# 32-bit matmuls with few moving columns, issued as two matmuls of 64 stationary columns each

## The chip, the cores and the metric

The kernel runs on one core of one Trainium2 chip. The metric is the time of one execution in device microseconds (us); lower is better. Nothing else runs on the chip, and all weights are read from HBM once per execution.

## The reference, cut to what matters

Two transformer blocks in float32 on 256 tokens of width 1024. Block one: SwiGLU, then a mixer (a pooling mixer and a retention with an RMS norm per head), then SwiGLU. Block two: a sliding-window attention with sinks (8 heads of 64) beside a three-branch sparse attention (compressed, selected and window keys), a gated merge, and a SwiGLU with a short convolution.

The change touches the TensorE side of these four expressions:

```python
# 1. retention: mean square of each head's output, for its RMS norm
o = o * lax.rsqrt(jnp.mean(o * o, axis=-1, keepdims=True) + EPS)
# 2. probabilities times values, of the window branch and both dense branches of the sparse attention
out = jnp.einsum('bgrqk,bkgd->bqgrd', probs.astype(v.dtype), vb)
# 3. scores of the queries on the compressed keys
lc = jnp.einsum('bqgrd,bcgd->bgrqc', qb, k_cmp) * scale
# 4. relative bias of the compressed scores: a bucket's one-hot times the table
lc = jnp.where(valid_c, lc + head_bias(table_gr, dist_c), NEG)
```

## The kernel before, in words

**Work and stages.** All weights stream through three slots of 1 MB each ("units"). SyncE loads a unit into `raw`; ScalarE writes its rounded half `w_hi` (L458, L465); VectorE writes the rest `w_lo = raw - w_hi` (L914, L931); TensorE multiplies. A big product is three fast 32-bit ("fp32r") matmuls of split operands (`passes`, L1562; `split_high` L1579 and `split_low` L1587; the row units, L1678). The stages are, in order: feed-forward 1 (0 to 197 us of the span), the mixer (to 290), feed-forward 2 (to 477), the attention block (to 650) and feed-forward 3.

**Order on TensorE.** The order is written out by hand: one instruction stream in program order, with semaphore waits. In the attention block, `for m in range(20)` goes over the weight units; each has two halves, and before a half the function `attend(k)` inserts pieces of attention work for position `k`. Eighteen "slots" of attention (3 branches, 6 slots each) go through a pipeline: `attend_scores` (L1918: scores, contraction over 64 rows, the two row halves `side` as separate matmuls), VectorE adds the bias and takes the maximum (L1257, L1263, L1266), ScalarE exponentiates (L643), `attend_turns` (L1930) transposes the probabilities, ScalarE copies them to SBUF (`prob_t`, L632), and `attend_values` (L1947) multiplies by the values.

**The matmuls that the change touches.** They are plain 32-bit matmuls on a full 128x128 array with few moving columns:

- `attend_values`, L1947: each slot has 4 matmuls with 64 moving columns, 18 slots, so 72 matmuls. The stationary operand is a 128x128 block of transposed probabilities, the output is 128 tokens by 64.
- The mean squares of the retention heads, L1868 (in the mixer, unit m = 9): 8 matmuls with 1 moving column (`mean_h`).
- The scores on compressed keys, L2060 (in the attention block, at (18, 0)): 8 matmuls with 32 moving columns.
- The bias of compressed scores, L1801 (in the first feed-forward, at about 22 us): 8 matmuls with 32 moving columns.

A plain 32-bit matmul of the program shows in the trace as two weight loads and two matmuls; one load with its matmul is called a pass below. So the four groups have 144, 16, 16 and 16 passes. The fp32r matmuls have one pass each. Other lines that matter: L1998 and L2000 are fp32r matmuls with 32 and 64 stationary columns on the first columns of the array; L2075 is a plain 32-bit matmul with 512 moving columns.

Of the kernel before, what the change touches and what calls it, by code (L numbers as in the profile page):

```python
# [31 lines left out]
P = 128  # L32
# [18 lines left out]
HD = 64  # L51
# [77 lines left out]
def build(nc, a, out):  # L129

    with ExitStack() as ctx:
# [69 lines left out]
        o_sq = sq[:, 0:HR]  # L201
# [1356 lines left out]
        def _(pe):  # L1558
# [226 lines left out]
            def bias_products():  # L1785

                pe.wait_ge(bias_in, 16 * 3)
                nc.tensor.matmul(acc[0:16, 1, 0:BIASW], bias_table, oh[:, OH_D0 - BIAS_D0:OH_D0 - BIAS_D0 + BIASW],
                                 start=True, stop=True).then_inc(bias_mm, 1)
                pe.wait_ge(vec_in, 16 * 10)  # L1790
                pe.wait_ge(conv_in, 16 * 4)
                nc.tensor.transpose(acc[:, 2, 0:V_ROWS], vec_rows[0:V_ROWS], ident[0:V_ROWS, 0:V_ROWS])
                for j in range(4):
                    mm = nc.tensor.transpose(acc[:, 2, P + 44 * j:P + 44 * (j + 1)], conv_rows[:, j],
                                             ident[0:44, 0:44])
                mm.then_inc(vec_turned, 1)
                pe.wait_ge(diag_in, 16 * 4)
                for b in range(2):
                    for g in range(4):
                        y0 = OH_D0 + P * b - 64 * g - 31  # L1800
                        mm = nc.tensor.matmul(acc[:, 3, P * b + 32 * g:P * b + 32 * (g + 1)], oh4[:, y0:y0 + P],  # L1801
                                              table_diag, start=True, stop=True)
                mm.then_inc(bias_cmp_mm, 1)

            pe.wait_ge(const_set, 3)
# [32 lines left out]
            for m in range(10):  # L1838
                u = U_MIX + m
                pe.wait_ge(lo_done, u + 1)  # L1840
                if m >= 2:
                    pe.wait_ge(proj_out, m - 1)
                bank = wk[:, m % 2]
                if m == 0:
                    first_unit(u % SLOTS, 1, False).then_inc(unit_done, 1)
                    continue
                for half in range(2):
                    if m in (6, 7):
                        mm = tok_tile(u % SLOTS, half, bank[:, half * T:(half + 1) * T], slice(0, UC))
                    else:  # L1850
                        mm = col_tile(u % SLOTS, half, bank[:, half * T:(half + 1) * T])
                    if half:
                        mm.then_inc(unit_done, 1)
                    elif m == 1:
                        spread(1, wk[:, 3, T:])
                    elif m in (6, 7):
                        scores(2 * m - 12)
                        scores(2 * m - 11)
                    elif m == 8:
                        for h in range(HR):  # L1860
                            head_out_mm(h)
                    elif m == 9:

                        pe.wait_ge(osq_out, 2)
                        for h in range(HR):
                            for tt in range(2):
                                n = 2 * h + tt
                                mm = nc.tensor.matmul(wk[:, 2, n:n + 1], o_sq[:, h, tt * P:(tt + 1) * P],  # L1868
                                                      mean_h[:], start=True, stop=True)
                        mm.then_inc(hms_ready, 1)  # L1870
                if m == 8:
                    pool_mix(0)
                    pool_mix(1)
# [59 lines left out]
            def attend_values(k):  # L1933
                for s in range(SLOTS_A):
                    if value_time(s) == k:
# [4 lines left out]
                        nh, h0, b = (2, 2 * w, 1) if w < 4 else (4, 4 * (w - 4), 0)  # L1940
                        for h in range(nh):
                            head = h0 + h
                            dst = wk[:, 3 - b, head * HD:(head + 1) * HD]
                            g = head // 4
                            for kc in range(b + 1):
                                n = h * (b + 1) + kc
                                mm = nc.tensor.matmul(dst, prob_t[s % 2][:, n * P:(n + 1) * P],  # L1947
                                                      v2[r % 2][:, kc, g * HD:(g + 1) * HD], start=kc == 0,
                                                      stop=kc == b)
                        mm.then_inc(pv_mm, 1)  # L1950

            def turn_values(n, bank):
# [14 lines left out]
            for m in range(20):  # L1967
# [20 lines left out]
                for half in range(2):  # L1988
# [65 lines left out]
                    if at == (18, 0):  # L2054
                        pe.wait_ge(kcz_ready, 1)
                        pe.wait_ge(y_lo, 2)
                        for b in range(2):
                            for j in range(4):
                                g = j // 2
                                mm = nc.tensor.matmul(acc[:, 2, b * P + 32 * j:b * P + 32 * (j + 1)],  # L2060
                                                      qb_s[:, j, b * P:(b + 1) * P], kcz[:, :, g * 16:(g + 1) * 16],
                                                      start=True, stop=True)
                        mm.then_inc(cscore_mm, 1)
                    if at == (19, 0):
                        pe.wait_ge(cprob, 1)
# [106 lines left out]
```

## Time and profile before

| what | value |
|---|---|
| median of 3 runs | 873.73 us (873.67 to 874.76) |
| the profiled execution, its own time | 872.87 us |
| its span in the trace | 871.1 us |
| TensorE matmul busy (PE) | 854.3 us, 98% |
| TensorE weight load busy (PEld) | 758.0 us, 87% |
| VectorE busy (DVE) | 646.3 us, 74% |
| ScalarE busy (ACT) | 444.4 us, 51% |
| TensorE clock granted, mean | 0.997 of full |

PE is a busy time of pipelined matmuls, so 98% says that there is nearly always one in flight, not how fast they follow each other. How fast they follow is read from groups of equal instructions: their stretch, less the duration of one, over their number less one. PEld is the weight load, which runs beside the matmuls. The execution's own time is 1.8 us longer than its span.

### The profile page before, as it was taken

Reading aid. Unit: us, or ns where it says so; the run is one execution under the profiler, and the core shown is the slowest. Engines: PE = TensorE matmul, PEld = TensorE weight load, DVE = VectorE, ACT = ScalarE, POOL = GpSimd, SP = SyncE. Lnnn points to the kernel's source line nnn. Section 1 sums busy time; section 2 is a strip of 40 time slices with the busy share of each in tenths; the row PEclk is TensorE's granted clock in tenths of the full one; section 3 lists DMA queues with packets and bytes.
Section 4 is the critical chain, followed back from the end, with each engine's and each line's share of the span. In section 5 each row is a group of like instructions: output and inputs, shape, how many; then the busy total and the mean of one; then the engine's idle time right before and its main releaser. Section 6 shows DMA issues by size and latency. Waiting matters only on the chain.

```text
span 871.1 us, 13695 instructions
## 1 busy us (share of the span) xinstructions
PE 854.3 (98%) x5275; PEld 758.0 (87%) x5275; DVE 646.3 (74%) x826; ACT 444.4 (51%) x564; POOL 72.0 (8%) x63
## 2 busy tenths in 40 slices
PE   8999999999999999999999999999999999999995
PEld 6888888889998888888888999889998988888884
DVE  5786766768767676766766867777766798998996
ACT  6445444445243645445445545666434555655652
POOL 1100000014321200000003301100003000000000
PEclk9999999999999999999999999999999999999998
DMA  8875665547744476665665753745546456466441
GB/s 234 321 243 189 193 194 191 191 146 222 214 146 134 134 247 234 217 221 188 191 179 160 165 153 110 194 112 137 188 146 193 146 179 207 144 218 216 144 169 49
DMA packets 119233, 158.10 MB, mean 181 GB/s; under 512 B 4572, under 2 KB 104332, under 8 KB 119068
## 3 DMA queue, kind: packets, MB, share of 16 engines
q1 hardware_dynamic: 116604, 151.19, 55.2%
q0 software_dynamic: 1488, 5.34, 1.8%
q10 hardware_dynamic: 1104, 1.05, 0.4%
q8 instruction: 26, 0.43, 0.2%
q14 instruction: 11, 0.09, 0.0%
HBM read 154.79 MB, written 1.07 MB: 179 GB/s over the span
## 4 chain that ended last, share of the span: by engine, by line
PE 75%; DVE 13%; issue 6%; ACT 4%; DMA 1%; ACTq 1%; DVEq 0%
PE wk L1562 20%; PE acc L1678 20%; PE wk L1579 18%; PE wk L1587 10%; DVE w_lo L931 4%; DVE work L1500 3%; DVE work L1490 1%; ACT work L736 1%; PE wk L1947 1%; DVE work L1487 1%; PE acc L1918 1%; PE acc L1595 1%; DMA x<-in_x 1%; DVE w_lo L914 1%; PE acc L1930 1%
## 5 line engine op out<-in xcount | busy, mean ns | idle before, releaser
L1579 PE MATMUL wk<-xhl,w_hi 128*128 128x512 f32 x992 | 239.2, 391 | 0.0
L931 DVE TENSOR_TENSOR w_lo<-raw,w_hi 128x2048 fp32r<-128x2048 f32 x83 | 190.0, 2289 | 64.1 <-ACT w_hi L465 62.9
L1579 PEld LDWEIGHTS wk<-xhl,w_hi 128*128 128x128 f32 x992 | 182.8, 188 | 35.8 <-ACT w_hi L488 0.3
L1562 PE MATMUL wk<-xhl,w_hi 128*128 128x256 f32 x896 | 166.3, 287 | 1.1 <-DVE w_lo L931 1.0
L465 ACT ACTIVATE w_hi<-raw 128x2048 fp32r<-128x2048 f32 x83 | 158.0, 1905 | 0.0
L1678 PE MATMUL acc<-w_hi,hhl 128*128 128x512 f32 x480 | 153.2, 390 | 0.0
L1562 PEld LDWEIGHTS wk<-xhl,w_hi 128*128 128x128 f32 x896 | 139.5, 191 | 3.6 <-issue 2.8
L458 ACT ACTIVATE w_hi<-raw 128x2048 fp32r<-128x2048 f32 x56 | 106.5, 1911 | 65.8 <-PE wk L1562 49.4
L1587 PEld LDWEIGHTS wk<-xhl,w_lo 128*128 128x128 f32 x992 | 129.3, 191 | 6.3
L914 DVE TENSOR_TENSOR w_lo<-raw,w_hi 128x2048 fp32r<-128x2048 f32 x49 | 114.4, 2337 | 23.4 <-ACT w_hi L458 23.2
L1587 PE MATMUL wk<-xhl,w_lo 128*128 128x256 f32 x992 | 131.1, 282 | 0.0
L1562 PE MATMUL wk<-xhl,w_lo 128*128 128x256 f32 x448 | 126.6, 283 | 0.0
L1678 PEld LDWEIGHTS acc<-w_hi,hhl 128*128 128x128 f32 x480 | 90.2, 188 | 18.4 <-issue 0.2
L1678 PE MATMUL acc<-w_lo,hhl 128*128 128x512 f32 x240 | 93.7, 390 | 0.0
L1562 PEld LDWEIGHTS wk<-xhl,w_lo 128*128 128x128 f32 x448 | 85.7, 191 | 0.0
L1678 PEld LDWEIGHTS acc<-w_lo,hhl 128*128 128x128 f32 x240 | 45.2, 188 | 8.3
L528 ACT ACTIVATE hhl<-work 128x512 fp32r<-128x512 f32 x20 | 12.7, 635 | 59.6 <-PE acc L1678 45.9
L736 ACT ACTIVATE work<-work,conv 128x256 f32<-128x256 f32 x44 | 24.2, 597 | 33.8 <-DVE work L1490 30.0
L513 ACT ACTIVATE work<-wk 128x512 f32<-128x512 f32 x22 | 13.2, 598 | 54.9 <-PE wk L1587 54.8
L791 POOL TENSOR_TENSOR w_lo<-raw,w_hi 128x1024 fp32r<-128x1024 f32 x4 | 9.6, 2391 | 380.5 <-DVE w_lo L921 380.5
L1500 DVE SCALAR_TENSOR_TENSOR work<-work,conv 128x255 f32<-128x255 f32 (+1 forms) x88 | 37.4, 479 | 1.9 <-ACT work L736 1.8
L1678 PE MATMUL acc<-w_hi,mhl 128*128 128x512 f32 x112 | 36.5, 395 | 1.1 <-DVE mhl L1537 1.1
(250 smaller groups left out, 948.2 us busy)
## 6 DMA issues: line engine op xcount, KB each, us to landing
raw<-in_ffn_w SPq DMA_DIRECT2D x65, 1024.0 KB, 5.3
raw<-in_w_in SPq DMA_DIRECT2D x26, 1024.0 KB, 7.1
raw<-in_w_ffn_in SPq DMA_DIRECT2D x22, 1024.0 KB, 5.1
raw<-in_w_ffn_out SPq DMA_DIRECT2D x11, 1024.0 KB, 4.9
raw<-in_w_out SPq DMA_DIRECT2D x8, 1024.0 KB, 5.0
arena<-bias_scratch POOLq DMA_DIRECT2D x4, 512.0 KB, 6.3
raw<-in_cmp_w_k SPq DMA_DIRECT2D x2, 1024.0 KB, 5.8
raw<-in_cmp_w_v SPq DMA_DIRECT2D x2, 1024.0 KB, 7.0
```

Source lines behind the costliest of these rows:

```text
L458: nc.scalar.activation(w_hi[:, u % SLOTS], raw[:, u % SLOTS], ACT.Copy).then_inc(hi_done, 1)
L465: nc.scalar.activation(w_hi[:, s], raw[:, s], ACT.Copy).then_inc(hi_done, 1)
L513: nc.scalar.activation(k_n(part, 2), wk[:, 0:2, T:2 * T], ACT.Copy).then_inc(a_low, 1)
L528: nc.scalar.activation(dst[:, 0:2], k_n(h_s, 2), ACT.Copy).then_inc(hh_out, 1)
L736: nc.scalar.activation(k_n(dst, 2)[:, t], k_n(src, 2)[:, t], ACT.Identity, scale=conv[:, 2, bass.ds(f, 1)], bias=conv[:, 3, bass.ds(f, 1)]) \
L914: nc.vector.tensor_tensor(w_lo[:, s], raw[:, s], w_hi[:, s].bitcast(F32), ALU.subtract) \
L931: nc.vector.tensor_tensor(w_lo[:, s], raw[:, s], w_hi[:, s].bitcast(F32), ALU.subtract) \
L1500: nc.vector.scalar_tensor_tensor(out=new, in0=tile[:, 0:T - back], scalar=conv[:, 2 - back, bass.ds(f, 1)], in1=new, op0=ALU.mult, op1=ALU ...
L1562: mm = nc.tensor.matmul(dst, w, v, start=start and n == 0, stop=stop and n == len(pairs) - 1, skip_group_check=True)
L1579: mm = nc.tensor.matmul(bank, wh[:, c, cols], xhl[:, c].rearrange("p n t -> p (n t)"), start=c == 0, stop=False, skip_group_check=True)
L1587: mm = nc.tensor.matmul(bank[:, 0:T], wl[:, c, cols], xh[:, c], start=False, stop=c == DC - 1, skip_group_check=True)
L1678: mm = nc.tensor.matmul(acc[:, b], w, v[:, c, cols], start=opens and c == 0 and n == 0, stop=end and n == 2, skip_group_check=True)
```

## The change

Each touched matmul becomes two, one for each half of its 128 stationary columns. Half `t0 = 0` loads stationary columns 0 to 63 and writes output partitions 0 to 63; half `t0 = 64` loads columns 64 to 127 and writes partitions 64 to 127, which puts it on the other 64 columns of the array. The moving operand is the same for both and is streamed for each. In every loop the two halves stand next to each other, as the two row halves do at L1918. Waits and increments stay where they were; the number of matmuls of the four groups goes from 96 to 192. No other engine's instructions change. (`HD` is 64, `P` is 128.)

```diff
                     for g in range(4):
                         y0 = OH_D0 + P * b - 64 * g - 31
-                        mm = nc.tensor.matmul(acc[:, 3, P * b + 32 * g:P * b + 32 * (g + 1)], oh4[:, y0:y0 + P],
-                                              table_diag, start=True, stop=True)
+                        for t0 in (0, HD):
+                            mm = nc.tensor.matmul(acc[t0:t0 + HD, 3, P * b + 32 * g:P * b + 32 * (g + 1)],
+                                                  oh4[:, y0 + t0:y0 + t0 + HD], table_diag, start=True, stop=True)
...
                             for tt in range(2):
                                 n = 2 * h + tt
-                                mm = nc.tensor.matmul(wk[:, 2, n:n + 1], o_sq[:, h, tt * P:(tt + 1) * P],
-                                                      mean_h[:], start=True, stop=True)
+                                for t0 in (0, HD):
+                                    toks = slice(tt * P + t0, tt * P + t0 + HD)
+                                    mm = nc.tensor.matmul(wk[t0:t0 + HD, 2, n:n + 1], o_sq[:, h, toks], mean_h[:],
+                                                          start=True, stop=True)
...
-                            dst = wk[:, 3 - b, head * HD:(head + 1) * HD]
+                            cols = slice(head * HD, (head + 1) * HD)
                             g = head // 4
                             for kc in range(b + 1):
                                 n = h * (b + 1) + kc
-                                mm = nc.tensor.matmul(dst, prob_t[s % 2][:, n * P:(n + 1) * P],
-                                                      v2[r % 2][:, kc, g * HD:(g + 1) * HD], start=kc == 0,
-                                                      stop=kc == b)
+                                for t0 in (0, HD):
+                                    mm = nc.tensor.matmul(wk[t0:t0 + HD, 3 - b, cols],
+                                                          prob_t[s % 2][:, n * P + t0:n * P + t0 + HD],
+                                                          v2[r % 2][:, kc, g * HD:(g + 1) * HD], start=kc == 0,
+                                                          stop=kc == b)
...
                             for j in range(4):
                                 g = j // 2
-                                mm = nc.tensor.matmul(acc[:, 2, b * P + 32 * j:b * P + 32 * (j + 1)],
-                                                      qb_s[:, j, b * P:(b + 1) * P], kcz[:, :, g * 16:(g + 1) * 16],
-                                                      start=True, stop=True)
+                                for t0 in (0, HD):
+                                    mm = nc.tensor.matmul(acc[t0:t0 + HD, 2, b * P + 32 * j:b * P + 32 * (j + 1)],
+                                                          qb_s[:, j, b * P + t0:b * P + t0 + HD],
+                                                          kcz[:, :, g * 16:(g + 1) * 16], start=True, stop=True)
```

The program's order on TensorE around one value group in the attention block, before (names as in the kernel; the last figures are output partitions by moving columns, and the count is of matmuls, not passes):

```order
L1562 MATMUL wk<-xhl,w_hi 128x256 x2
L1562 MATMUL wk<-xhl,w_lo 128x256
L1918 MATMUL acc<-arena 128x256 x2
L1930 MATMUL acc<-cst,arena 128x128 x4
L1947 MATMUL wk<-arena 128x64 x4
L1562 MATMUL wk<-xhl,w_hi 128x256 x2
```

and of the change, at the same place:

```order
L1562 MATMUL wk<-xhl,w_hi 128x256 x2
L1562 MATMUL wk<-xhl,w_lo 128x256
L1921 MATMUL acc<-arena 128x256 x2
L1933 MATMUL acc<-cst,arena 128x128 x4
L1951 MATMUL wk<-arena 64x64 x8
L1562 MATMUL wk<-xhl,w_hi 128x256 x2
```

Nothing moved past anything: four matmuls became eight of half the width at the same place, and lines after the edits are numbered 3 to 6 higher.

## Rows read from the trace of the kernel before

**Rows 1.** The page: busy time of each engine, share of the span, instructions.
```profile
PE 854.3 (98%) x5275; PEld 758.0 (87%) x5275; DVE 646.3 (74%) x826; ACT 444.4 (51%) x564; POOL 72.0 (8%) x63
```
**Rows 2.** Waits of TensorE's matmuls: waited for; us in total, times, longest.
```profile
PE wk L1947 <- ACT arena L632: 2.0, 2, 1.3
```
**Rows 3.** Chain that ended last, in time: start us, us, what.
```profile
22.26 1.90 PE acc L1801 x16
...
260.59 1.68 PE wk L1868 x16
...
511.83 0.84 PE wk L1947 x8
...
566.45 1.10 PE wk L1947 x8
...
597.50 0.84 PE wk L1947 x8
...
615.73 1.71 PE acc L2060 x16
...
626.36 1.72 PE acc L2075 x4
```
**Rows 4.** Timeline of weight loads: start us, us, engine, line, out<-in, rows*columns, form, count.
```profile
260.31 1.88 PEld L1868 LDWEIGHTS wk<-mean_h,sq 128*128 128x128 f32 x16
...
558.94 0.97 PEld L1947 LDWEIGHTS wk<-arena 128*128 128x128 f32 x8
559.98 0.52 PEld L1918 LDWEIGHTS acc<-arena 64*128 64x128 f32 x8
```
**Rows 5.** Groups of weight loads by form: busy us, mean ns of one.
```profile
L1947 PEld LDWEIGHTS wk<-arena 128*128 128x128 f32 x144 | 17.5, 192 | 2.4 <-ACT arena L632 2.4
...
L2000 PEld LDWEIGHTS wk<-w_hi,mhl 128*64 128x64 f32 x32 | 4.3, 135 | 0.2
L1998 PEld LDWEIGHTS wk<-w_lo,mhl 128*32 128x32 f32 x32 | 3.5, 108 | 1.6 <-issue 1.3
```
**Rows 6.** Timeline of weight loads, 593 to 595 us: full array to 32 columns.
```profile
593.24 0.97 PEld L1947 LDWEIGHTS wk<-arena 128*128 128x128 f32 x8
594.13 0.11 PEld L1998 LDWEIGHTS wk<-w_lo,mhl 128*32 128x32 f32 x1
594.19 0.14 PEld L2000 LDWEIGHTS wk<-w_hi,mhl 128*64 128x64 f32 x1
...
594.90 0.13 PEld L2000 LDWEIGHTS wk<-w_hi,mhl 128*64 128x64 f32 x1
595.02 0.26 PEld L1930 LDWEIGHTS acc<-cst,arena 128*128 128x128 f32 x2
```
**Rows 7.** Timeline of weight loads, 525 to 527 us: full array to row halves and back.
```profile
525.15 0.19 PEld L1562 LDWEIGHTS wk<-xhl,w_lo 128*128 128x128 f32 x1
525.48 0.52 PEld L1918 LDWEIGHTS acc<-arena 64*128 64x128 f32 x8
526.12 0.42 PEld L1930 LDWEIGHTS acc<-cst,arena 128*128 128x128 f32 x4
```
**Rows 8.** Timeline of VectorE, weight loads and ScalarE, 24 to 36 us.
```profile
26.84 2.29 DVE L914 TENSOR_TENSOR w_lo<-raw,w_hi 128x2048 fp32r<-128x2048 f32 x1 [1.61 <-ACT w_hi L458]
29.05 0.42 DVE L988 COPY rstd_b<-acc 128x256 f32<-128x256 f32 x1
...
35.09 0.69 DVE L1037 TENSOR_TENSOR hhl<-work,hhl 128x512 fp32r<-128x512 f32 x1 [0.70 <-ACT hhl L528]
...
35.86 0.19 PEld L1678 LDWEIGHTS acc<-w_hi,hhl 128*128 128x128 f32 x1 [0.22 <-issue]
...
24.89 1.92 ACT L458 ACTIVATE w_hi<-raw 128x2048 fp32r<-128x2048 f32 x1 [2.14 <-DMA raw<-in_ffn_w]
```
**Rows 9.** Timeline of VectorE and of weight loads at 520 us.
```profile
517.99 2.28 DVE L914 TENSOR_TENSOR w_lo<-raw,w_hi 128x2048 fp32r<-128x2048 f32 x1
...
520.49 0.52 PEld L1918 LDWEIGHTS acc<-arena 64*128 64x128 f32 x8
```

## The prediction

> **What bounds the kernel now.** I read the page first [rows 1]. A matmul is in flight for 98% of the span and a weight load for 87%, while VectorE and ScalarE have a quarter and a half of it free. The waits of TensorE's matmuls name ScalarE's copy L632 in front of the value group L1947 as the largest, with only 2.0 us [rows 2]. So time taken out of TensorE's stream should come off the end, wherever the stream is what the rest waits for. The chain that ended last says where that is [rows 3]: it holds the mean squares (1.68 us), the compressed scores (1.71 us) and 14 of the 18 value groups, 12 of 0.84 us and the two behind a wait of 1.10 us. It passes by four value groups (in the trace at 530.7, 534.5, 561.9 and 579.4 us), where it runs over VectorE or ScalarE instead.
>
> **What sets the pace of a touched group** is the weight load. The 16 loads of the mean squares take 1.88 us and one lasts 0.192: (1.88 - 0.192)/15 = 0.112 us per pass, with 1 moving column. The 8 loads of a value group, with 64 moving columns, give (0.97 - 0.192)/7 = 0.111 [rows 4]. Between 1 and 64 moving columns nothing changes, so what counts is that 128 stationary columns are loaded, twice per matmul. A load of 128 columns lasts 192 ns, one of 64 columns 135, one of 32 columns 108 [rows 5]: 0.89 and 0.84 ns per column. Half as many columns save 57 ns, and 112 - 57 = 55 ns is what a pass of a half could take.
>
> **The change, step by step.** It removes 96 matmuls of 128 stationary columns (192 passes) and adds 192 of 64 (384 passes). If the halves take turns, two of 55 ns cost what one of 112 did. The whole gain hangs on both halves loading and streaming at the same time.
>
> The nearest row that shows such a thing is L1918, the scores, as two row halves side by side. Its 8 loads of the full 128 columns take 0.52 us, against 0.97 us for the 8 of L1947 [rows 4]. That is four pairs, (0.52 - 0.188)/3 = 0.111 us per pair: two loads in the time of one. The new code puts its halves next to each other in the same way, so that the two can be paired. The stream does not stand in the way: four passes of 512 moving columns in plain 32 bits take 1.72 us [rows 3], 0.84 ns per column, and 64 columns so 54 ns, no more than the load's 55.
>
> I take the paired case: 112 - 55, and a little of it kept back, so 55 ns saved per old pass.
> - Value groups: 14 on the chain, of 8 passes: 14 x 8 x 0.055 = 6.2 us. The four that are not on the chain give nothing; there TensorE only waits longer.
> - Mean squares and compressed scores: 2 x 16 x 0.055 = 1.8 us.
> - Bias of the compressed scores: 16 passes, 0.9 us in TensorE's stream, taken as nothing, though the chain names it. Behind it TensorE resumes with L1678 at 35.86 us, which waited for `hhl` (L1037), ended at 35.78. That goes back over L1013 to `rstd_b`, L988, which stood in VectorE's queue behind the `w_lo` of 26.84 to 29.13 us; this waited for ScalarE's `w_hi`, and that for a weight transfer [rows 8]. This cover is VectorE's and the transfer's; it is already what ends the wait, so no loss below about 0.3 us would show there either.
> - What comes back: at 520.27 us `w_lo` is ready 0.22 us before TensorE wants it [rows 9]. Two value groups before it save 0.44 us each and only the first can move VectorE's work too, so some 0.2 us are lost. Further on, with 18 slots closer together, the softmax on VectorE and ScalarE may be late more often than the two waits of rows 2; I allow 0.6 us for it.
>
> Sum: 6.2 + 1.8 - 0.8 = 7.2 us. The profiled execution took 872.87 us, so 865.7 on its account; it lies 0.9 under the median of 873.73, and 873.7 - 7.2 = 866.5 is what I give. The unknown price is what a pair costs. From below, the shortest that load and stream allow, 54 ns, and nothing lost: 14 x 8 x 0.058 + 32 x 0.058 = 8.4 us, 865.3. From above, halves that take turns at 58 ns: 0.6 us lost. I take the end near the row halves, because these are the same engine, the same plain 32-bit passes, and the same order in the program.
>
> **Whether switching the array costs.** Going from the full array to row halves has a visible price. Between loads of L1562 lie 0.12 us, but from the last of them to L1918 it is 525.48 - 525.15 = 0.33, so 0.21 more; and out again, from the last pair (526.00 - 0.19 = 525.81) to 526.12, 0.31 where a pass takes 0.11 [rows 7]. For column parts no such price shows: from the last L1947 load to L1998 with 32 columns it is (594.13 - 593.24) - 7 x 0.111 = 0.11, and from 64 columns back to 128 another 0.12 [rows 6]. So I book nothing. The Trainium skill, TensorEngine Tiling (Array Packing), Tiling Modes, says that a change of tiling mode, not of tile alone, drains the engine; the row halves agree, the column rows do not. But those columns are always the first ones of the array, and no row shows the second half in use.
>
> **The rivals.**
> 1. *The halves run in pairs, but each group pays for entering and leaving* as row halves do. In: 0.21 us. Out: 0.15 to 0.20, the lower figure from 1.04 us for a value group in front of L1918 against 0.89 in front of L1998 [rows 4, 6]. Seven of the 14 value groups stand in front of L1918 and pay 0.15 already. Price: 7 x 0.24 + 7 x 0.39 + 2 x 0.4 = 5.2 us, of the gain of 7.2. Result 871.7. For it: the second half is new. Against it: rows 6.
> 2. *The change doesn't do what it says: the halves take turns.* Either the two weight loads share one path, or one half's load waits for the other half's matmul, or the instructions don't arrive fast enough. In the row pairs 16 instructions come in about 0.5 us, some 30 ns each; four per 55 ns are twice as many. Then a pass costs 110 to 116 ns as two halves: 0 to 0.6 us more over the 144 passes on the chain, 873.7 to 874.3. For it: row halves read different partitions for their weights, while column halves both read all 128; nothing in this trace shows two loads from the same partitions at once. The Trainium skill, TensorE: Matmul & The Clock Gate, Part 3, says that weight loads overlap matmuls in flight only when their row group differs, and column halves share it; the row halves agree, as far as they go.
> 3. *Slower: they take turns and the array pays for each switch.* Place: all 16 groups on the chain. Price: the 5.2 us of rival 1, on top of 0.6: 879.5. It decides from the point where the pair gains less than the switch costs, for a value group 0.4 us, or 50 of the 55 ns per pass. Against it: it needs both doubts at once.
>
> **How the numbers follow.** The forecast has 0.45, rival 1 has 0.15, rival 2 has 0.26, rival 3 has 0.14. Likeliest, and so the predicted time, is 866.5 us, with a range of its own of 865.3 to 869.0. The range for 8 in 10 takes in the forecast, rival 1 and rival 2: 865.2 to 874.6. It leaves out rival 3 and the ends of the others. A measurement of this kernel can tell about 0.2% from no change, 1.7 us. The forecast and rival 1 are faster by more: 0.60. Rival 2 is within it: 0.26. Rival 3 is slower: 0.14.
>
> **What would show it.** In the changed profile, a value group should be 16 weight loads of 64 columns in about 0.5 us (0.135 + 7 x 0.055 = 0.52); if its stretch is 0.9 to 1.0 us, rival 2 holds. The mean squares should go from 1.88 to about 1.0 us. The load behind a value group should follow within 0.06 to 0.12 us, and the first load of a group within 0.12 us of the load before it; gaps of 0.3 us are rival 1 or 3. The stretch of feed-forward 1 should not move. If the value groups are as short as said and the time is still over 869, then the wait before L1947 or before L1930 has grown, and my 0.8 us were too small.

## The result, and the profile after

The changed kernel takes 869.14 us (median of 5 runs, 868.62 to 870.69), the kernel before 874.55 on the same chip (5 runs, 873.67 to 875.35). The ratio is 0.9943, with a 95% interval of 0.9929 to 0.9958: faster by 3.7 to 6.2 us. The forecast was 866.5 us; 869.14 lies in the range for 8 in 10 (865.2 to 874.6), but just above the forecast's own (865.3 to 869.0).

The page of the kernel after, busy time of each engine, answers to [rows 1]. TensorE has 3.1 us of matmuls less, weight loads 7.0 us less; the other engines are where they were.

```profile
PE 851.2 (98%) x5463; PEld 751.0 (86%) x5467; DVE 645.9 (74%) x826; ACT 444.0 (51%) x564; POOL 71.9 (8%) x63
```

The waits of TensorE's matmuls, after (waited for; us in total, times, longest), answer to [rows 2]. The wait in front of the values grew by 0.4 us in all. Two smaller ones, in front of L1960 and of the transposes, grew by 0.2 us each.

```profile
PE wk L1951 <- ACT arena L632: 2.4, 2, 1.4
...
PE acc L1960 <- DVE sq L1228: 0.8, 1, 0.8
...
PE acc L1933 <- ACT arena L643: 0.5, 2, 0.3
```

The same two lines before, where L1960 was L1955 and L1933 was L1930:

```profile
PE acc L1955 <- DVE sq L1228: 0.6, 1, 0.6
PE acc L1930 <- ACT arena L643: 0.3, 1, 0.3
```

The chain that ended last, after (start us, us, what), answers to [rows 3]. Bias, mean squares and compressed scores went from 1.90, 1.68 and 1.71 us to 1.06, 1.03 and 1.06. The 512-column group L2081, which the change leaves alone, still takes 1.72.

```profile
22.43 1.06 PE acc L1802 x32
...
260.29 1.03 PE wk L1871 x32
...
614.11 1.06 PE acc L2066 x32
...
624.20 1.72 PE acc L2081 x4
```

The weight loads in time, after (start us, us, engine, line, out<-in, rows*columns, form, count), answer to [rows 4, 6, 7]. They hold the result.

```profile
259.89 0.19 PEld L1562 LDWEIGHTS wk<-xhl,w_lo 128*128 128x128 f32 x1
260.22 1.01 PEld L1871 LDWEIGHTS wk<-mean_h,sq 128*64 128x64 f32 x32
261.25 0.30 PEld L1562 LDWEIGHTS wk<-xhl,w_hi 128*128 128x128 f32 x2
...
515.23 0.42 PEld L1933 LDWEIGHTS acc<-cst,arena 128*128 128x128 f32 x4 [0.33 <-issue]
515.82 0.55 PEld L1951 LDWEIGHTS wk<-arena 128*64 128x64 f32 x16 [0.17 <-issue]
516.43 0.30 PEld L1562 LDWEIGHTS wk<-xhl,w_hi 128*128 128x128 f32 x2
...
560.51 0.55 PEld L1951 LDWEIGHTS wk<-arena 128*64 128x64 f32 x16 [0.17 <-issue]
561.12 0.52 PEld L1921 LDWEIGHTS acc<-arena 64*128 64x128 f32 x8
```

- **The halves run in pairs.** Sixteen loads of a value group take 0.55 us, where eight of the full width took 0.97 [rows 4]. One load lasts 0.138, so a pair costs (0.55 - 0.138)/7 = 0.059 us instead of a pass of 0.112.
- **And the array is switched for them.** From the load before the mean squares to their first one it is 260.22 - 259.89 = 0.33 us, where a pass takes 0.12: 0.21 more, as for row halves [rows 7]. The transposes in front of a value group take 515.82 - 515.23 = 0.59 us from first load to first load of what follows; before it was 0.39. Behind the values the single loads give 0.206 us from the last to the next, where before it was 0.112 in front of L1562 and 0.26 in front of the scores.
- So a value group and its transposes took 0.39 + 0.89 = 1.28 us and now take 0.59 + 0.61 = 1.20: **0.08 us gained**. In front of the scores it is 0.39 + 1.04 against 0.59 + 0.61: **0.23 gained**. Without the switch it would be some 0.43 (8 passes of 0.112 less 8 pairs of 0.059).

### The profile page after: what moved, and what is told of

Same layout as the page of the kernel before. It is cut to its first block, busy times and chain, and to the rows that moved or that the text cites. A ratio compares the mean times of both kernels' runs of the same rounds, so it can differ in the third digit from the quotient of the medians.

```text
span 868.9 us, 14075 instructions
## 1 busy us (share of the span) xinstructions
PE 851.2 (98%) x5463; PEld 751.0 (86%) x5467; DVE 645.9 (74%) x826; ACT 444.0 (51%) x564; POOL 71.9 (8%) x63
## 4 chain that ended last, share of the span: by engine, by line
PE 75%; DVE 13%; issue 6%; ACT 3%; DMA 1%; ACTq 1%; DVEq 0%
PE wk L1562 20%; PE acc L1678 20%; PE wk L1579 18%; PE wk L1587 10%; DVE w_lo L931 4%; DVE work L1500 3%; DVE work L1490 1%; ACT work L736 1%; DVE work L1487 1%; PE acc L1921 1%; PE wk L1951 1%; PE acc L1933 1%; PE acc L1595 1%; DMA x<-in_x 1%; DVE w_lo L914 1%
## 5 line engine op out<-in xcount | busy, mean ns | idle before, releaser
L1562 PE MATMUL wk<-xhl,w_hi 128*128 128x256 f32 x896 | 167.7, 288 | 1.0 <-DVE w_lo L931 0.9
L1678 PE MATMUL acc<-w_hi,hhl 128*128 128x512 f32 x480 | 153.2, 390 | 0.4 <-issue 0.4
L1562 PEld LDWEIGHTS wk<-xhl,w_hi 128*128 128x128 f32 x896 | 140.6, 193 | 4.2 <-issue 2.9
L1562 PE MATMUL wk<-xhl,w_lo 128*128 128x256 f32 x448 | 127.1, 284 | 0.0
L1678 PEld LDWEIGHTS acc<-w_hi,hhl 128*128 128x128 f32 x480 | 90.2, 188 | 18.7 <-issue 0.5
L1678 PE MATMUL acc<-w_lo,hhl 128*128 128x512 f32 x240 | 93.7, 390 | 0.0
L1562 PEld LDWEIGHTS wk<-xhl,w_lo 128*128 128x128 f32 x448 | 86.3, 193 | 0.0
L1678 PEld LDWEIGHTS acc<-w_lo,hhl 128*128 128x128 f32 x240 | 45.2, 188 | 8.2
L1678 PE MATMUL acc<-w_hi,mhl 128*128 128x512 f32 x112 | 36.5, 396 | 1.1 <-DVE mhl L1537 1.1
```

Of the source, the lines that this page charges most:

```text
L1562: mm = nc.tensor.matmul(dst, w, v, start=start and n == 0, stop=stop and n == len(pairs) - 1, skip_group_check=True)
L1678: mm = nc.tensor.matmul(acc[:, b], w, v[:, c, cols], start=opens and c == 0 and n == 0, stop=end and n == 2, skip_group_check=True)
```

## Experiments

### One half alone: does the second half bring the switch?

Only one half of the values is computed, so these two leave out tokens 64 to 127 (first kernel) or 0 to 63 (second) of each block in the probabilities times values. Everything else is the changed kernel. The edit of the first; the second has `(HD,)`:

```diff
-                                for t0 in (0, HD):
+                                for t0 in (0,):
                                     mm = nc.tensor.matmul(wk[t0:t0 + HD, 3 - b, cols],
```

> This kernel leaves out the second halves (output tokens 64 to 127) of the value matmuls; the other three groups keep both halves. Theory A (a pair runs side by side, and the array pays for every entry and exit of column halves): the stretch from the first load of a value group to the load behind it stays at 0.61 us, as with both halves, because a pair costs what one costs. If entering costs are tied to the halves as such, the gap in front of the group stays at 0.31 us behind transposes and the gap behind it at 0.21. Rival B (the price is paid only for using the second half of the array, since 64 columns on the first half already stood in the kernel before without a gap): the gaps shrink to 0.11 us and the group takes 0.42 to 0.46 us. Rival C (two halves take turns with loads of some 26 ns each): the group's eight passes would take half as long, about 0.2 us plus gaps.

> This kernel leaves out the first halves (output tokens 0 to 63) of the value matmuls. Theory A: as with the first halves alone, 0.61 us per value group, gaps of 0.31 in front and 0.21 behind. Rival B: here the gaps are back at 0.31 and 0.21 us, while with the first halves alone they are 0.11. Rival C: eight passes in about 0.2 us plus gaps.

Measured: 870.36 and 870.44 us, one run each, beside 872.51 for the kernel before; the changed kernel's own profiled run took 870.69. The weight loads of the first, at a group in front of the scores:

```profile
559.57 0.48 PEld L1933 LDWEIGHTS acc<-cst,arena 128*128 128x128 f32 x4
560.21 0.54 PEld L1951 LDWEIGHTS wk<-arena 128*64 128x64 f32 x8 [0.17 <-issue]
560.82 0.52 PEld L1921 LDWEIGHTS acc<-arena 64*128 64x128 f32 x8
```

From their first load to the next group eight loads take 0.61 us, sixteen 0.61 as well (561.12 - 560.51, above), and in the trace of the second half alone it is again 0.61. So the other half costs nothing: a pair costs what one costs. The idle 0.17 in front is there with the first 64 columns alone. So it isn't the second half of the array that costs: the doubt that I had about [rows 6], that those columns are always the first ones, was the wrong one.

### The halves one after the other: what pairs them?

```diff
-                        for h in range(nh):
-                            for kc in range(b + 1):
-                                for t0 in (0, HD):
+                        for t0 in (0, HD):
+                            for h in range(nh):
+                                for kc in range(b + 1):
                                     mm = nc.tensor.matmul(wk[t0:t0 + HD, 3 - b, cols],
```

> All value matmuls of the first half of a group are issued before all of the second half; nothing else differs from the change. Theory A with pairing by neighbourhood (the engine takes instructions in order and only neighbours on different halves run together): 16 passes of 52 ns one after the other, so a value group takes about 0.83 us plus the gap behind it, 1.03 in all, and the time is some 14 x 0.4 = 5.6 us above the change's, about 874.5. Rival (the engine reaches ahead and pairs them from a distance): the group stays at 0.61 us and the time at 869.

Measured: 872.31 us (one run), 0.2 under the kernel before. Its weight loads:

```profile
558.11 0.46 PEld L1933 LDWEIGHTS acc<-cst,arena 128*128 128x128 f32 x4
558.74 0.83 PEld L1951 LDWEIGHTS wk<-arena 128*64 128x64 f32 x16 [0.17 <-issue]
559.63 0.52 PEld L1921 LDWEIGHTS acc<-arena 64*128 64x128 f32 x8
```

The same sixteen loads take 0.83 us instead of 0.55. The single loads follow one another at 55 to 58 ns; only around the turn, where the last three of the first half meet the first of the second, do they fall together (559.025 and 559.027, 559.082 and 559.083, 559.137 and 559.142). So halves pair up with near neighbours in the program, a few instructions away. A group now takes 559.63 - 558.74 = 0.89 us, 0.28 more than in pairs, where the expectation had 0.4 more. Laid beside the trace of the kernel before, by the loads of lines that neither changes, this one loses 1.3 us over the value groups (the switches, with nothing gained for them) and gains 0.65 by 36 us, 0.6 at the mean squares and 0.5 at the compressed scores. Over the value groups it so lies 3.5 us above the changed kernel's undisturbed trace (last experiment), and not 5.6: the gap behind the group was counted too large, and the groups count whether they are among the 14 or not. The mechanism is the one that was named.

### The kernel before, again: how much do its own runs differ?

> The kernel before, unchanged, for a second profile. The first profile of it was 872.87 us, below all its timed runs (873.67 to 875.35), and the change's profile 870.69, above all its others (868.62 to 869.91). If the traces' difference of 2.2 us understates the change because of a stretch at half clock that only some executions have, this profile shows 873.5 to 875 us, and more time than the first one between 0 and 36 us or between 560 and 572 us, with everything else within 0.1 us of it. If instead it is 872.9 again, the timed runs carry something that profiled ones don't.

Measured: 874.19 us, the same program that took 872.51 in the same comparison. Its weight loads behind the bias:

```profile
22.36 1.86 PEld L1801 LDWEIGHTS acc<-arena 128*128 128x128 f32 x16
24.14 2.38 PEld L1579 LDWEIGHTS wk<-xhl,w_hi 128*128 128x128 f32 x8
26.61 1.94 PEld L1587 LDWEIGHTS wk<-xhl,w_lo 128*128 128x128 f32 x8
...
28.93 1.69 PEld L1579 LDWEIGHTS wk<-xhl,w_hi 128*128 128x128 f32 x8
30.67 1.13 PEld L1587 LDWEIGHTS wk<-xhl,w_lo 128*128 128x128 f32 x8
```

The same eight loads take 2.38 and 1.69 us, 1.94 and 1.13. The clock tells why. Busy time by stretch of this run (us, busy of PE, PEld, DVE, ACT, POOL, then granted clock, DMA share, GB/s):

```profile
22.00:36.00 14.00, 14.00 (x78) 12.35 (x78) 11.14 (x22) 6.03 (x7) 2.38 (x7) 0.88 1.06 379
562.00:572.00 10.00, 8.71 (x75) 7.83 (x73) 7.85 (x16) 7.21 (x23) 0.00 (x0) 1.00 0.45 123
```

The mean over these 14 us is 0.88, so part of them ran at the lower level, 1.2 GHz: the rows right behind the bias group. In the first profile of the kernel before it was 1.00 there. TensorE was busy for all of the 14.00 us. L1678 starts 1.4 us later than in [rows 8]. The changed kernel's profiled run has such a stretch elsewhere:

```profile
562.00:572.00 10.00, 8.34 (x76) 7.12 (x74) 6.21 (x11) 9.04 (x23) 0.00 (x0) 0.83 0.55 150
```

There TensorE had stood for 1.45 us in front of L1951, waiting for ScalarE's copy, and had then run the values and the scores. Matmuls of the changed kernel, timeline of PE:

```profile
565.17 0.69 PE L1951 MATMUL wk<-arena 128*64 128x64 f32 x16 [1.45 <-ACT arena L632]
...
567.13 0.41 PE L1562 MATMUL wk<-xhl,w_lo 128*128 128x256 f32 x1
...
569.68 0.28 PE L1562 MATMUL wk<-xhl,w_lo 128*128 128x256 f32 x1
```

The same matmul lasts 0.41 us in the stretch and 0.28 behind it. Each of the 14 profiles of this study holds none or one such stretch, worth 1.3 us behind the bias and 1.5 at 565 us: seven none, one (this one) behind the bias, six between 565 and 572 us. Those six stand behind a wait of 1.3 or 1.45 us in front of the values, but seven more profiles have that wait and no stretch behind it, so the wait alone does not bring it on.

The timed runs have no trace, but each has its mean granted clock on record. The 36 runs of the kernel before, over all comparisons, fall into three groups: 8 at 872.4 to 872.7 us, all with 0.997; 21 at 873.8 to 874.4, with 0.994 to 0.997; 7 at 875.0 to 876.0, with 0.992 to 0.995. The groups lie 1.4 to 1.5 us apart, the price of one stretch, so they fit none, one and two stretches in a run; that they are this is likely and not shown, as the mean also holds the half clock behind TensorE's last matmul, which differs from run to run. The median of a kernel thus depends on how many of its runs hold a stretch. This must be kept apart from the change.

### The values alone, all but the values, and the bias alone

Each puts the original lines back for the rest. For the first, the bias, the mean squares and the compressed scores are whole again:

```diff
-                        for t0 in (0, HD):
-                            mm = nc.tensor.matmul(acc[t0:t0 + HD, 3, P * b + 32 * g:P * b + 32 * (g + 1)],
-                                                  oh4[:, y0 + t0:y0 + t0 + HD], table_diag, start=True, stop=True)
+                        mm = nc.tensor.matmul(acc[:, 3, P * b + 32 * g:P * b + 32 * (g + 1)], oh4[:, y0:y0 + P],
+                                              table_diag, start=True, stop=True)
...
```

> Only the value matmuls are in halves; mean squares, compressed scores and bias are whole, as before. By the stretches in the change's profile a value group in front of L1562 or L2003 saves 0.08 us and one in front of L1921 0.22 us, the dearer turn in front of it counted in: some 2.1 us over the 14 on the chain. Theory D (what the stretches show is all there is): 2.1 us under the kernel before, a ratio of 0.9976. Theory E (the executions of the kernel before mostly carry a stretch at half clock behind the whole bias group, as its second profile does, worth some 1.4 us, which halves of the bias take away): the same 2.1 us here, since the bias is whole, and the missing 1.4 us only where the bias is in halves. Some executions may lose 1.2 us at 565 us, behind the longer wait there.

> The value matmuls are whole again; mean squares, compressed scores and bias are in halves. Theory D: 0.56 + 0.54 us from the first two, nothing from the bias: 1.1 us under the kernel before, ratio 0.9987. Theory E: 1.1 and some 1.4 us, 2.5 us under, ratio 0.9971.

> Only the bias of the compressed scores is in halves. Theory D (the wait for the gated hidden tile hides it): within 0.3 us of the kernel before. Theory E (the whole group of 16 passes is what the clock falls behind): about 1.4 us under the median of the kernel before, ratio 0.9984, the granted clock 1.0 between 22 and 36 us, and L1579 behind the group at 0.22 us per load throughout.

| kernel | median, us (runs) | lowest | ratio, 95% interval |
|---|---|---|---|
| before, same chip | 874.14 (15) | 872.65 | |
| values in halves, the rest whole | 871.47 (5) | 870.24 | 0.9960, 0.9946 to 0.9973 |
| all but the values in halves | 871.32 (5) | 870.91 | 0.9961, 0.9948 to 0.9975 |
| bias alone in halves | 872.43 (11) | 872.14 | 0.9980, 0.9971 to 0.9989 |

The two parts add up: 2.7 and 2.8 us, 5.5 together, against 5.4 for the whole change. The values' 2.7 is above the 2.1 that both theories gave; their lowest run is 2.4 under, and the traces give 2.3 (last experiment). The bias is worth 1.7 us between the medians, near the 1.4 of theory E and not within the 0.3 of theory D, and no single trace explains it. In the trace of the bias alone, TensorE resumes at 35.48 us:

```profile
22.37 1.01 PEld L1802 LDWEIGHTS acc<-arena 128*64 128x64 f32 x32
23.42 1.68 PEld L1579 LDWEIGHTS wk<-xhl,w_hi 128*128 128x128 f32 x8
25.14 1.13 PEld L1587 LDWEIGHTS wk<-xhl,w_lo 128*128 128x128 f32 x8
...
35.48 0.19 PEld L1678 LDWEIGHTS acc<-w_hi,hhl 128*128 128x128 f32 x1 [0.40 <-issue]
```

It is 0.38 us earlier than before [rows 8]. But with the values alone, where the bias is whole, it resumes at 35.27, with no idle time ahead. The same load there:

```profile
35.27 0.19 PEld L1678 LDWEIGHTS acc<-w_hi,hhl 128*128 128x128 f32 x1
```

The tile that it needs, VectorE's `hhl` (L1037), was ready there at 35.05. So in that execution TensorE's own stream ended last, and not the cover that the prediction read from the first trace. Where the bias group starts varies by 0.7 us among the profiles (21.90 to 22.58), and where `w_hi` starts behind its weight transfer by 1.4 (23.46 to 24.89), so one pair of traces says little. Counted from the first load of the bias to L1678, it is 13.67 and 13.37 us in the two profiles with the bias whole and no stretch behind it, and 12.91 to 13.27 in the eleven with the bias in parts. The lowest runs point the same way: the bias alone is 0.5 us under the kernel before, and all but the values 1.7, where mean squares and compressed scores give 1.1 in the traces. So a direct gain of about half a us is likely; two profiles with the bias whole are too few to show it.

The rest of the 1.7 us would be the half-clock stretch behind the bias: of three profiles with the bias whole one has it, of eleven with the bias in parts none. Of the runs of the bias alone 6 of 11 lie in a lowest group, 872.14 to 872.43, of the kernel before 1 of 15 in this comparison, though 5 of 11 in another. That it is why the medians differ by more than the lowest runs is likely, but not shown: no timed run has a trace.

### Quarters: do the instructions arrive fast enough?

All four groups are issued as four quarters of 32 stationary columns.

```diff
-                                for t0 in (0, HD):
-                                    mm = nc.tensor.matmul(wk[t0:t0 + HD, 3 - b, cols],
-                                                          prob_t[s % 2][:, n * P + t0:n * P + t0 + HD],
+                                for t0 in range(0, P, 32):
+                                    mm = nc.tensor.matmul(wk[t0:t0 + 32, 3 - b, cols],
+                                                          prob_t[s % 2][:, n * P + t0:n * P + t0 + 32],
...
```

> All four groups as quarters of 32 stationary columns, on the array's four column quarters. Theory A: the four quarters run side by side. A load of 32 columns lasts 27 ns less than one of 64 and sets the pace where few columns move: mean squares (1 column) and compressed scores (32 columns, 27 ns of stream) go from 0.052 to about 0.03 us per pass, 0.35 us less for each group; the value groups, with 64 columns streaming for 54 ns, stay at 0.61 us. Together about 0.7 us under the change, 868.4. Rival (instructions come too slowly: eight per pass instead of four): the groups get longer, at about 7 ns per instruction 0.056 us per pass and so no gain, at 15 ns 0.12 us per pass and a time above that of the kernel before.

Measured: 868.30 us (867.80 to 869.20, 5 runs), ratio 0.9929 (0.9916 to 0.9943). The weight loads:

```profile
259.92 0.63 PEld L1871 LDWEIGHTS wk<-mean_h,sq 128*32 128x32 f32 x64
260.56 0.30 PEld L1562 LDWEIGHTS wk<-xhl,w_hi 128*128 128x128 f32 x2
...
559.55 0.49 PEld L1951 LDWEIGHTS wk<-arena 128*32 128x32 f32 x32 [0.17 <-issue]
560.13 0.52 PEld L1921 LDWEIGHTS acc<-arena 64*128 64x128 f32 x8
```

With 1 moving column, four quarters take (0.63 - 0.108)/15 = 0.035 us: 128 instructions in some 0.6 us, 5 ns each. So the doubt of rival 2 about the rate of instructions is gone. With 64 moving columns, four quarters take (0.49 - 0.108)/7 = 0.055 us, no less than the stream of 64 columns, 54 ns in the prediction. The values were near that floor with halves already: a group takes 560.13 - 559.55 = 0.58 us in place of 0.61. Laid beside the second trace of the changed kernel (last experiment), mean squares and compressed scores gain 0.4 us each, as expected, the values 0.35, for which nothing was expected, and by 36 us 0.1.

### The two fast groups with column parts in plain 32 bits: who pays the switch?

L2003 and L2005 are the fp32r matmuls that [rows 6] rest on. Here the same operands are read as plain 32 bits, nothing else is changed.

```diff
-                            nc.tensor.matmul(wk[0:32, 1, v * T:(v + 1) * T], blk_hl[0][:, v, j0 + j], wl[:, j],
+                            nc.tensor.matmul(wk[0:32, 1, v * T:(v + 1) * T], blk_hl[0][:, v, j0 + j].bitcast(F32),
+                                             wl[:, j].bitcast(F32),
...
```

> The change, but the 32- and 64-column matmuls on compression weights (L2003 and L2005), which are fp32r and pay nothing for entering, run as plain 32-bit matmuls of the same values, still on the first columns of the array. Theory F (a switch is paid by plain 32-bit matmuls on part of the columns, not by fp32r ones): the gap in front of such a group grows from 0.11 to about 0.31 us, the gap behind it to 0.2 us or more, and possibly each change between 32 and 64 columns costs a gap too. Rival G (what is paid for is something about the value groups, such as two halves being in use in the program): these groups still follow without a gap. Either way two passes in place of one, and 256 columns at the plain rate (0.21 us each), make the eight groups of matmuls some 2.5 us longer each: near 880 us.

Measured: 893.86 us (one run). Its weight loads:

```profile
545.94 0.14 PEld L2003 LDWEIGHTS wk<-w_lo,mhl 128*32 128x32 f32 x2 [0.39 <-issue]
546.49 0.19 PEld L2005 LDWEIGHTS wk<-w_hi,mhl 128*64 128x64 f32 x2 [0.41 <-issue]
547.06 0.14 PEld L2003 LDWEIGHTS wk<-w_lo,mhl 128*32 128x32 f32 x2 [0.39 <-issue]
```

In fp32r the loads of L2003 and L2005 follow each other by 0.12 us [rows 6]. In plain 32 bits each change between 32 and 64 columns takes 546.49 - 545.94 = 0.55 us and 0.57, most of it idle. Two passes of 256 moving columns need 2 x 256 x 0.84 = 0.43 us of stream by the price of L2081; the load of the next group doesn't run beside it, as it does everywhere else, but starts behind it. So the switch exists for column parts of plain 32-bit matmuls and not for those of fp32r, and a change of the number of columns is one, too. The time is 20 us above the kernel before and 24 above the changed kernel's 870. The expectation's 880 was also added up wrongly: eight groups at its own 2.5 us give 20 on top of the changed kernel, 889. The other direction, the values in fp32r, wasn't tried.

### Values beside the scores: the price of one edge

At positions before 8, the values are moved from behind the transposes to a place between scores and transposes, first in quarters, then in halves.

```diff
                 if k < 8:
                     attend_scores(k)
-                attend_turns(k)
-                attend_values(k)
-                if k >= 8:
+                    attend_values(k)
+                    attend_turns(k)
+                else:
+                    attend_turns(k)
+                    attend_values(k)
                     attend_scores(k)
```

> Quarters in all four groups, and for the first eight positions of the attention (before weight unit 8) the value group stands right behind the scores and in front of the transposes, so that the array goes row halves, column quarters, full, in place of row halves, full, column quarters, full. Theory A (each change between full array, row parts and column parts costs some 0.2 us once): one change fewer at the four positions that hold scores, transposes and values, 0.8 us under the quarters, 867.5. Rival (row to column costs two switches, or the transposes that now come later push the softmax out): no gain, 868.3 or a little above.

> The changed kernel with one difference: at the positions before 8 the values come right behind the scores and before the transposes. At four positions scores and values then stand side by side, row halves and column halves. Theory (a switch is priced per edge, 0.2 us in and 0.2 out, and an edge from row halves to column halves costs both): each of the four positions loses nothing on the edge scores to values, and the edge transposes to values (0.2 us) is gone, so 0.8 us less than the changed kernel, 868.3 +- 0.4. Rival (an edge between two parts of the array is free): 0.4 more at each, 866.7. Rival (earlier values let the copies and the softmax start late or early): a wait before the transposes, no gain or a loss, 869.1 or more.

Measured in quarters: 866.94 us (866.48 to 869.00, 6 runs), ratio 0.9928 (0.9914 to 0.9942) against 873.99 of the kernel before there. In halves: 868.08 us (867.95 to 869.36, 5 runs), ratio 0.9938 (0.9924 to 0.9952), beside 869.93 for the changed kernel on the same chip; the spans of the two profiles, neither with a half-clock stretch, are 866.3 and 867.1: 0.8 us, as expected. The weight loads, halves:

```profile
509.05 0.19 PEld L1562 LDWEIGHTS wk<-xhl,w_lo 128*128 128x128 f32 x1
509.37 0.30 PEld L1923 LDWEIGHTS acc<-arena 64*128 64x128 f32 x4
510.01 0.55 PEld L1953 LDWEIGHTS wk<-arena 128*64 128x64 f32 x16 [0.33 <-issue]
510.62 0.42 PEld L1935 LDWEIGHTS acc<-cst,arena 128*128 128x128 f32 x4
511.01 0.30 PEld L1562 LDWEIGHTS wk<-xhl,w_hi 128*128 128x128 f32 x2
```

Scores, values and transposes take 0.64, 0.61 and 0.39 us: 1.64, where the changed kernel needs 0.63 + 0.59 + 0.61 = 1.83. The edge transposes to values, 0.2 us, is gone at four positions, since the values enter where the array has just been changed anyway. The quarters in this order are the fastest kernel of the study; their lowest run is 1.3 us under that of quarters in the old order. The traces show 0.8 of it at the same four positions; the other 0.5, between two comparisons, no trace explains.

### The changed kernel, again: mechanism and clock apart

> The changed kernel, unchanged, timed again beside the kernel before. Theory G (the change takes 3.6 to 4.0 us out by its mechanism, the rest of the 5.4 us between the medians is half-clock stretches of about 1.2 us, of which the kernel before has one or two in most runs and the changed kernel fewer): the fastest runs of the two kernels differ by 3.6 to 4.2 us (about 868.5 against 872.5), the medians by 4.5 to 5.5. Theory H (all of it is the mechanism, and my accounting from the traces misses 1.5 us): the fastest differ by as much as the medians, 5 us or more.

Measured: 869.93 us (868.92 to 871.70, 5 runs), ratio 0.9958 (0.9944 to 0.9972) to 874.16 of the kernel before there (872.68 to 875.99, 9 runs). The lowest runs differ by 3.8 us, as the first theory has it, the medians by 4.2, less than its 4.5. This profiled run has the clock at 1.00 where the first one had 0.83:

```profile
562.00:572.00 10.00, 8.34 (x87) 6.91 (x86) 6.90 (x13) 8.77 (x22) 0.00 (x0) 1.00 0.53 144
```

Its span is 867.1 us, against 871.1 of the kernel before, also undisturbed. The two traces, laid side by side by the loads of untouched lines, part as follows: 0.48 us by 36 us (the bias and the scatter of the transfers, which no trace parts), 0.60 at the mean squares, 2.28 over the value groups, 0.54 at the compressed scores; 3.9 us in all, and 0.1 in the rest. The change itself is worth at least the last three, 3.4 us; how much of the 0.48 is the bias stays open (above).

## Why the prediction was right or wrong

- **What bounds the kernel**: right. What was saved in TensorE's stream behind 36 us came off the end, but for 0.5 us that went into longer waits; other engines' times are unchanged.
- **The price of a pair**: 55 ns saved per old pass were booked. Measured 112 - 59 = 53. The halves run together, as the row halves did, and rivals 2 and 3 fell with the first profile. The Trainium skill, TensorE: Matmul & The Clock Gate, Part 3, has loads overlap matmuls in flight only with another row group. Here both halves read the same 128 rows, and still a half alone and a pair take the same 0.61 us; the measurement decides.
- **"Whether switching the array costs. ... So I book nothing"**: this is the step that failed. Each touched group pays 0.2 us for going in, and 0.15 behind it in front of L1562 (0.206 where a pair takes 0.059); in front of the scores one edge of 0.206 takes the place of one of 0.26. A value group so gains 0.08 or 0.23 us instead of the 0.44 booked. I had read the column rows of [rows 6] as the nearer ones, because they were column parts; but they are fp32r, and the touched matmuls are plain 32 bits, like the row halves of [rows 7]. The format was the nearer likeness. The Trainium skill, TensorEngine Tiling (Array Packing), Tiling Modes, says that changing the mode, not just the tile, drains the engine. By the runs that holds for plain 32-bit column parts, at 0.2 us going in and 0.1 to 0.15 coming out, and not for fp32r ones, at nothing visible.
- **The value groups**: 14 x 8 x 0.055 = 6.2 us booked, 2.28 measured. Nine groups stand in front of scores and nine in front of other work; 9 x 0.23 + 9 x 0.08 = 2.8 us would come off if none were covered, and the waits kept 0.5. "The four that are not on the chain give nothing" was wrong as well: laid side by side, the traces part at those four groups too, by 0.08, 0.08, 0.23 and 0.22 us. It was a small error beside the switch.
- **Mean squares and compressed scores**: 1.8 us booked, 0.60 + 0.54 = 1.1 measured, the difference being their two switches, 0.2 us in and 0.1 out each.
- **Bias**: nothing booked. It is worth 1.7 us between the medians and 0.5 between the lowest runs. The cover read from [rows 8] was 0.2 us thin in that execution and absent in another, so booking nothing was too strict; the rest is probably the half-clock stretch behind it, of which the prediction knew nothing.
- **What comes back**: 0.8 us booked. The waits grew by 0.4 + 0.2 + 0.2 us [rows 2], the same sum; laid side by side, the traces lose 0.5 of it over the value groups.
- **Rival 1** is what happened. It gave 871.7 from 873.7, a gain of 2.0 us; the undisturbed traces give 3.4. Its prices held: 0.24 and 0.39 us a value group, where 0.44 - 0.23 = 0.21 and 0.44 - 0.08 = 0.36 were measured. What it lacked is 0.5 us of the values, where it let four groups give nothing, the 0.8 that it took off for what comes back, and 0.1 in the other two groups.

Of the 5.4 us between the medians (4.2 in the second comparison), 3.4 are the mechanism's at mean squares, values and compressed scores, less than half of the 7.2 that were booked. The lowest of all runs of the two kernels, 868.62 and 872.44, are 3.8 apart, 0.4 more than those 3.4, and that is likely the bias's. The rest is more or fewer half-clock stretches in a run, and scatter; how it divides stays open. That the median fell so near the forecast's own range is luck: the switch took back more than half of the gain, and the bias and the stretches gave some 2 us that no term had. Whether the changed kernel keeps TensorE from these stretches or merely falls otherwise is open too: the bias alone had one at 568 us in code that was the same as before.

## What to carry to other kernels

Two matmuls on disjoint column parts of the array run side by side if they stand next to each other, so a matmul with few moving columns costs the loading of its part; near the stream's time (64 columns, 54 ns) smaller parts bring little more. Price the edges of such a group first, 0.2 us in and 0.1 to 0.2 out, for plain 32-bit matmuls: a group of eight passes hardly pays for them, one of sixteen does, and groups with parts belong next to each other. When looking for the nearest row for an unknown price, match the number format before the shape.

## What the runs showed of the hardware that was not expected

- Column parts of plain 32-bit matmuls cost a switch, also for columns 0 to 63 alone (0.17 us idle), and also between 32 and 64 columns (0.55 us per group of two). The same parts in fp32r follow at 0.12.
- From row halves straight to column halves, 0.33 us of idle loads stand, the same 0.33 as from row halves to the full array. So it is one switch and not two, and what is saved is the edge into the column halves.
- Four loads of 32 columns went out within 20 ns (559.548 to 559.568 in the quarters), and the whole group of mean squares at 5 ns per instruction.
- TensorE's clock falls to 1.2 GHz for a few us in some executions and not in others of one and the same program: in six profiles behind a wait of 1.3 to 1.45 us, in one with no idle time of its matmuls ahead. Each costs 1.3 to 1.5 us, a quarter to a third of what this change brings.
